# A macaron encoder block on 8 cores: modulation and first weights taken piece by piece at the start, norm products taken in pairs, and pairs of squares added on GpSimd in nine norms

## The reference, cut to what matters

```python
mod = (cc @ w_ada[l] + b_ada[l]).reshape(b, N_ADA, D_MODEL)
sh1, sc1, gt1, sh2, sc2, gt2, sh3, sc3, gt3 = [mod[:, i, None, :] for i in range(N_ADA)]
h = modulate(rms_norm(x, g_ffn1[l]), sh1, sc1)
x = x + 0.5 * gt1 * swiglu(h, w_ffn1_in[l], w_ffn1_out[l])
h = modulate(rms_norm(x, g_mix[l]), sh2, sc2)
x = x + gt2 * token_mix(h, w_in[l], ...)
h = modulate(rms_norm(x, g_ffn2[l]), sh3, sc3)
x = x + 0.5 * gt3 * swiglu(h, w_ffn2_in[l], w_ffn2_out[l])
```

## Time and profile before

| | us |
|---|---|
| three runs | 1567.2, 1570.02, 1849.1 |
| median | 1570.02 |
| the profiled execution: its time | 1571.91 |
| its span, slowest core (core 1) | 1570.4 |
| its span, fastest core (core 0) | 1558.5 |
| TensorE matmuls busy, of the span | 1497.1 |
| VectorE busy | 809.7 |
| ScalarE busy | 448.9 |
| GpSimd busy, DMA issues counted | 78.4 |

### The profile page before, as it was taken

How to read it: one execution, slowest core, us unless ns; L and a number is a source line. 1 busy time by engine, 2 the same in 40 slices (tenths; PEclk the granted TensorE clock), 3 DMA queues, 4 the chain that set the end, 5 groups by cost and what they waited for, 6 DMA issues and landing times.

```text
span 1570.4 us, 23354 instructions; the slowest of 8 cores (1558.5 to 1570.4 us)
## 1 busy us (share of the span) xinstructions
PE 1497.1 (95%) x8372; PEld 708.4 (45%) x8372; DVE 809.7 (52%) x1310; ACT 448.9 (29%) x636; POOL 78.4 (5%) x152
## 2 busy tenths in 40 slices
PE   2689999999999999988999999999999999999998
PEld 1334444444444444454564445444444444444443
DVE  2264527254272656667875568745544626253644
ACT  3361010101101036548665454523511010101010
POOL 1000000000101000000001000001000000000000
PEclk9789999999999999999999999999999999999999
DMA  9943352523515311240025345345232121211022
GB/s 198 204 110 54 54 88 41 95 41 54 95 27 93 63 18 64 81 98 5 11 68 88 61 94 110 68 69 111 43 54 41 31 51 27 48 27 28 1 107 107
DMA packets 24302, 107.12 MB, mean 68 GB/s; under 512 B 2816, under 2 KB 3072, under 8 KB 21760
## 3 DMA queue, kind: packets, MB, share of 16 engines
q0 software_dynamic: 21312, 75.67, 28.2%
q1 hardware_dynamic: 2880, 29.98, 5.3%
HBM read 168.71 MB, written 12.58 MB: 115 GB/s over the span
## 4 chain that ended last, share of the span: by engine, by line
PE 88%; DMA 6%; DVE 2%; ACT 2%; issue 1%; DVEq 0%; ACTq 0%; SPq 0%; POOLq 0%
PE ps L663 42%; PE ps L691 21%; PE ps L1016 7%; PE ps L826 4%; PE ps L1029 3%; PE ps L1048 3%; DMA arena<-w1i 3%; DMA arena<-x 2%; PE ps L962 1%; PE ps L809 1%; PE ps L872 1%; PE ps L908 1%; ACT arena L485 1%; DVE arena L497 1%; PE ps L580 1%
## 5 line engine op out<-in xcount | busy, mean ns | idle before, releaser
L663 PE MATMUL ps<-arena 128*128 128x512 bf16 x3152 | 694.7, 381 | 12.9 <-DMA arena<-w1i 4.8
L485 ACT ACTIVATE arena<-ps 128x512 bf16<-128x512 f32 (+3 forms) x426 | 268.7, 652 | 975.6 <-PE ps L663 810.3
L663 PEld LDWEIGHTS ps<-arena 128*128 128x128 bf16 x3152 | 308.1, 98 | 385.4 <-issue 23.1
L491 DVE TENSOR_TENSOR arena<-arena,ps 128x512 bf16<-128x512 bf16 x198 | 135.4, 687 | 510.8 <-PE ps L663 490.8
L497 DVE SCALAR_TENSOR_TENSOR arena<-ps,arena 128x512 f32<-128x512 f32 (+1 forms) x500 | 359.7, 748 | 72.2 <-ACT arena L485 23.1
L691 PE MATMUL ps<-arena 128*128 128x512 bf16 x1584 | 345.2, 379 | 2.1 <-DVE arena L497 1.1
L691 PEld LDWEIGHTS ps<-arena 128*128 128x128 bf16 x1584 | 154.3, 98 | 189.2 <-issue 6.3
L491 DVE TENSOR_TENSOR arena<-arena 128x1024 bf16<-128x1024 bf16 (+9 forms) x180 | 114.5, 656 | 39.8 <-ACT arena L485 33.2
L1016 PE MATMUL ps<-arena 128*128 128x512 bf16 x512 | 116.0, 379 | 0.0
L485 ACT ACTIVATE arena<-arena 128x512 f32<-128x512 f32 (+2 forms) x86 | 89.4, 1054 | 43.7 <-DVE arena L497 23.1
L497 DVE SCALAR_TENSOR_TENSOR arena<-arena 128x512 f32<-128x512 f32 (+1 forms) x112 | 79.2, 739 | 20.8 <-ACT arena L485 9.7
(11 more groups left out here) (60 smaller groups left out, 500.6 us busy)
## 6 DMA issues: line engine op xcount, KB each, us to landing
arena<-w_ada POOLq DMA_DIRECT2D x36, 512.0 KB, 7.3
arena<-w_gate POOLq DMA_DIRECT2D x24, 512.0 KB, 6.6
arena<-w1i POOLq DMA_DIRECT2D x22, 512.0 KB, 5.4
arena<-w3i POOLq DMA_DIRECT2D x22, 512.0 KB, 5.1
arena<-x SPq DMA_DIRECT2D x5, 2048.0 KB, 16.3
outT<-arena SPq DMA_DIRECT2D x8, 1024.0 KB, 3.9
arena<-w1o POOLq DMA_DIRECT2D x10, 512.0 KB, 5.3
arena<-w_kqvu POOLq DMA_DIRECT2D x10, 512.0 KB, 6.4
```

The costliest lines, as they stand in the source:

```text
L485: return e.activation(out=o, in_=i, func=func, scale=scale)
L491: return e.tensor_tensor(out=out() if callable(out) else out, in0=in0() if callable(in0) else in0, in1=in1() if callable(in1) else in1, op=op)
L663: ins = e.matmul(pst(t), lhsT=w[:, kt, :], rhs=hk(b, kt), start=(kt == 0), stop=(kt == 7))
```

## The change

Five things change.

1. The start. `w1i` piece 0 is asked for ahead of `w_ada` pieces 6 and 7 (`W1ST`). Each of the eight `w_ada` pieces has its own PSUM tile, bias addition and two-column result in `SS1`; the four shift pieces are copied, the four scale pieces get `(1 + scale) * g`. After each scale piece two tiles of block 0 are modulated (`norm_late(0, (2k, 2k+1))`). The first unit alternates its two accumulations over `kt`, so it can begin with the tiles that are there. Group 0 of feed-forward 1 takes the units of blocks 0 and 1 in turn for each weight, and the norm of block 2 stands behind the second weight. `x` of block 3 is asked for when `w1i` piece 2 has landed, not piece 3. One ring place is skipped.

2. `norm_apply` takes two `kt` in one `tensor_tensor` of 128x1024 (x times `rs`), into buffers twice as large, and then scale and shift for each `kt` in one instruction: `kt` 1, 4 and 7 on ScalarE, the other five on VectorE.

3. In the nine norms with `sub` above 0 (`fold`), each half of four squares is added pairwise by one GpSimd `tensor_tensor` of 128x1024 bf16, and each half is then summed by two matmuls in place of four.

4. The planner's model of DMA landing times (a function `drain`, not shown: while both queues have work, SP gets `SPSHARE` of the bandwidth `BW` and POOL the rest), and 15 of the 18 pairs of `RAMPS`.

5. The last 16 tokens of block 0's `H` are copied once (`HH`), and the pooling stage reads them there (not shown).

```diff
@@ -19,11 +19,11 @@
 CELL = 32
 
 SILU, EXP, LN, TANH = "silu", "exp", "ln", "tanh"
-RAMPS = {"v0a": (7.37, 11.91), "k0a": (10.15, 10.65), "k0b": (10.89, 11.92), "v0b": (12.65, 12.7),
-         "a0": (10.37, 12.62), "u0": (10.3, 12.44), "k3": (11.93, 12.42), "k4": (11.01, 13.72),
-         "v3": (15.11, 15.16), "v4": (12.45, 12.73), "q4": (13.4, 13.6), "a1": (14.08, 16.26),
-         "g0": (13.99, 15.41), "o0": (16.97, 17.82), "u1": (15.03, 18.92), "g1": (20.0, 20.5),
-         "n1": (18.67, 20.59), "o1": (21.26, 21.31)}
+RAMPS = {"v0a": (6.86, 12.16), "k0a": (10.15, 11.87), "k0b": (10.76, 11.77), "v0b": (12.6, 12.7),
+         "a0": (10.39, 12.64), "u0": (10.68, 12.89), "k3": (11.4, 12.42), "k4": (11.01, 14.15),
+         "v3": (15.11, 15.16), "v4": (13.29, 13.34), "q4": (13.4, 13.6), "a1": (14.08, 16.3),
+         "g0": (13.99, 15.41), "o0": (17.33, 18.34), "u1": (15.09, 18.95), "g1": (19.52, 20.02),
+         "n1": (16.9, 20.3), "o1": (21.22, 21.31)}
...
@@ -53,6 +53,8 @@
     LAT = 0.12
     PELAT = 0.22
     WINDOW = 96
+    BW = 315e3
+    SPSHARE = 0.64
...
-    TMPS = [[view(o + 2048 * i, F32, (TB,)) for i in range(2)] for o in (o_qt, o_expb)]
+    SS1 = view(o_aq, F32, (2, 4, 8))
+
+    def twin(o, o2):
+        v = view(o, F32, (TB,))
+        return bass.AP(v.tensor, v.offset, [list(v.ap[0]), [(o2 - o) // 4, 2], [1, TB]])
+    TMPS = [[twin(o_qt, o_qt + 2048), twin(o_expb + 8192, o_att + 8192)],
+            [twin(o_expb, o_expb + 2048), twin(o_expb + 8192, o_kq)]]
...
-    def norm_stats(b):
+    def norm_stats(b, fold=False):
         t = Tile()
         for hf in range(2):
             sq = H[:, b, 4 * hf:4 * hf + 4, :]
@@ -574,12 +596,19 @@
         for hf in range(2):
             sq = H[:, b, 4 * hf:4 * hf + 4, :]
 
-            def mm(e, hf=hf):
+            nq = 4
+            if fold:
+                nq = 2
+                lo, hi = H[:, b, 4 * hf:4 * hf + 2, :], H[:, b, 4 * hf + 2:4 * hf + 4, :]
+                sq = lo
+                tt(lo, lo, hi, ALU.add, [lo, hi], [lo], 2.3, eng="pool")
+
+            def mm(e, hf=hf, nq=nq):
                 ins = None
-                for kt in range(4 * hf, 4 * hf + 4):
-                    ins = e.matmul(pst(t), lhsT=ONES, rhs=hk(b, kt), start=(kt == 0), stop=(kt == 7))
+                for kt in range(4 * hf, 4 * hf + nq):
+                    ins = e.matmul(pst(t), lhsT=ONES, rhs=hk(b, kt), start=(kt == 0), stop=(kt == 3 + nq))
                 return ins
-            S.op("pe", mm, reads=[sq, ONES] + ([t] if hf else []), writes=[t], cost=mmc(4, 512))
+            S.op("pe", mm, reads=[sq, ONES] + ([t] if hf else []), writes=[t], cost=mmc(nq, 512))
         rs = RK[rk_pos[0] % 2]
         rk_pos[0] += 1
         act(rs, lambda: pst(t), AF.Ln, bias=EPSC[:, 0:1], reads=[t, EPSC], writes=[rs], cost=0.69, tset=LN)
@@ -587,16 +616,22 @@
         return rs
 
     def norm_apply(b, sub, rs):
-        for kt in range(8):
+        sc, sh = DER[:, 3 * sub, :], DER[:, 3 * sub + 1, :]
+        for kp in range(4):
             tb = TMPS[0 if sub < 2 else 1][tmp_pos[0] % 2]
             tmp_pos[0] += 1
-            stt(tb, xk(b, kt), DER[:, 3 * sub, kt:kt + 1], rs, ALU.mult, ALU.mult,
-                [xk(b, kt), rs, DER[:, 3 * sub, :]], [tb], 0.75)
-            if kt % 2 == 0:
-                act(hk(b, kt), tb, AF.Identity, bias=DER[:, 3 * sub + 1, kt:kt + 1], reads=[tb, DER[:, 3 * sub + 1, :]],
-                    writes=[hk(b, kt)], cost=0.72)
-            else:
-                ts(hk(b, kt), tb, DER[:, 3 * sub + 1, kt:kt + 1], ALU.add, [tb, DER[:, 3 * sub + 1, :]], [hk(b, kt)], 0.49)
+            xp = xblk(b)[:, 2 * kp:2 * kp + 2, :]
+            rb = bass.AP(rs.tensor, rs.offset, [list(rs.ap[0]), [0, 2], [1, TB]])
+            tt(tb, xp, rb, ALU.mult, [xp, rs], [tb], 1.1)
+            for kt in (2 * kp, 2 * kp + 1):
+                ti = tb[:, kt % 2, :]
+                s1, s2 = sc[:, kt:kt + 1], sh[:, kt:kt + 1]
+                if kt in (1, 4, 7):
+                    act(hk(b, kt), ti, AF.Identity, bias=s2, scale=s1, reads=[ti, sc, sh], writes=[hk(b, kt)], cost=0.8)
+                else:
+                    S.op("dve", lambda e, kt=kt, ti=ti, s1=s1, s2=s2: e.tensor_scalar(
+                        out=hk(b, kt), in0=ti, scalar1=s1, scalar2=s2, op0=ALU.mult, op1=ALU.add),
+                        reads=[ti, sc, sh], writes=[hk(b, kt)], cost=0.49)
 
     def norm_early(b):
         rs = norm_stats(b)
...
-    def norm_late(b):
-        for kt in range(8):
+    def norm_late(b, kts):
+        for kt in kts:
             xs = XSE[b][:, kt, :]
-            sc, sh = DER[:, 0, kt:kt + 1], DER[:, 1, kt:kt + 1]
+            cells = [SS1[:, 0, kt // 2, :], SS1[:, 1, kt // 2, :]]
+            sc, sh = [c[:, kt % 2:kt % 2 + 1] for c in cells]
             if kt % 3 == 1:
                 S.op("act", lambda e, kt=kt, xs=xs, sc=sc, sh=sh: e.activation(out=hk(b, kt), in_=xs, func=AF.Identity,
                                                                               bias=sh, scale=sc),
-                     reads=[xs, DER[:, 0:2, :]], writes=[hk(b, kt)], cost=0.8)
+                     reads=[xs] + cells, writes=[hk(b, kt)], cost=0.8)
             else:
                 S.op("dve", lambda e, kt=kt, xs=xs, sc=sc, sh=sh: e.tensor_scalar(
                     out=hk(b, kt), in0=xs, scalar1=sc, scalar2=sh, op0=ALU.mult, op1=ALU.add),
-                    reads=[xs, DER[:, 0:2, :]], writes=[hk(b, kt)], cost=0.49)
+                    reads=[xs] + cells, writes=[hk(b, kt)], cost=0.49)
 
     def norm(b, sub):
-        norm_apply(b, sub, norm_stats(b))
-
-    for c in range(8):
+        norm_apply(b, sub, norm_stats(b, sub > 0))
+
+    for c in range(6):
         ada_load(c)
+    W1ST = load("s", w1i[0])
+    ada_load(6)
+    ada_load(7)
     norm_early(0)
     norm_early(1)
-    t_ada = Tile()
     for c in range(8):
-        ada_mm(c, t_ada, 0)
-    ada_out(t_ada, 0, 8)
+        t = Tile()
+        ada_mm(c, t, c)
+        ada_out(t, c, 1)
+        src = MOD[:, 2 * c:2 * c + 2]
+        k = c % 4
+        dst = SS1[:, 1 - c // 4, k, 0:2]
+        if c < 4:
+            S.op("dve", lambda e, src=src, dst=dst: e.tensor_copy(out=dst, in_=src), reads=[src], writes=[dst], cost=0.17)
+        else:
+            g = CST[:, 80 + 2 * k:82 + 2 * k]
+            S.op("dve", lambda e, src=src, dst=dst, g=g: e.scalar_tensor_tensor(
+                out=dst, in0=src, scalar=1.0, in1=g, op0=ALU.add, op1=ALU.mult), reads=[src, CST], writes=[dst], cost=0.17)
+            norm_late(0, (2 * k, 2 * k + 1))
+    norm_late(1, range(8))
...
@@ -712,23 +763,33 @@
                     r.append(load(ring, wo_dd[wo_pos + q], None if full else 1, deps)[0])
                 return r
             if bmajor:
-                wl = [load(ring, wi_d[GSTART[g] + jl]) for jl in range(nk)]
+                head = [W1ST] if first and g == 0 else []
+                wl = head + [load(ring, wi_d[GSTART[g] + jl]) for jl in range(len(head), nk)]
                 wts = [w[0] for w in wl]
                 if lastg:
                     wos = wo_load()
                 if first and g == 0:
-                    norm_late(0)
-                    norm_late(1)
-                    for b, after in ((2, ADA[7][1]), (3, wl[3][1]), (4, wl[3][1])):
+                    for b, after in ((2, ADA[7][1]), (3, wl[2][1]), (4, wl[3][1])):
                         xl[b] = S.op("sp", lambda e, b=b: e.dma_start(out=XB[:, b - 1, :, :],
                                                               in_=x_d[b].rearrange("p (k t) -> p k t", k=8)),
                              writes=[XB[:, b - 1, :, :]], dma="d_x%d" % b, nbytes=1 << 21, deps=[after])
                     wos = wo_load([xl[2]])
                     for c in range(8, 12):
+                        if c == 11:
+                            rpos["s"] += 1
                         ada_load(c, [xl[3]])
                 for i, b in enumerate(blocks):
                     if g == 0 and first:
-                        if 0 < i < len(blocks) - 1:
+                        if i == 0:
+                            for jl in range(nk):
+                                unit(jl, 0, wts[jl])
+                                unit(jl, 1, wts[jl])
+                                if jl == 1:
+                                    norm(2, 0)
+                            continue
+                        if i == 1:
+                            continue
+                        if i < len(blocks) - 1:
```

52 lines of the change are left out of this document (35 added, 17 removed).

## The result

The changed kernel takes **1543.9 us** (median of four runs, 1543.7 to 1544.8), the kernel before, run beside it, 1568.1 (mean of three, 1567.2 to 1570.0). The ratio is 0.9846, with a 95% interval of 0.9827 to 0.9866: some 24 us less. Predicted was 1542, with a range of 1535 to 1552. The gain is under 2%, to which the prediction gave a chance of 0.77. Disturbed runs are left out of every time in this text, so that the kernel before has three runs here and e10 two.

The account below looks back on a forecast made before the run. TensorE, busy 95%, bounds the kernel, so only its idle time and removed matmuls give time: 16.0 + 7.8 + 3.0 + 1.6 = 28.4 us off 1571.9 gives 1543.5, less 1.9 over the median: 1542, range 1535 to 1552.

Parts of the forecast that it names:

- The start: Reordered weight pieces bring group 0's output products at 128.6 against 144.65: 16.0 us gained.
- The cores differ now mostly by when the start ends: Across cores: differences come mostly from when the start ends, which the new start evens out; no size given.
- the 17 that would have been wrong: Sign of a wrong prediction: TensorE idle more than 17 us from 560 to 1120.
- Rival B: Start: block 3's `x` lands no earlier, at 81, so the start gives 12 to 13: 1545; chance 0.15.
- The sums: Nine norms lose four matmuls each, 36 x 0.216 = 7.8 us, with 18 POOL additions in their place.
- Where the addition is hidden: End of feed-forward 1, blocks 0 to 2: an addition of 2.3 us is hidden with 0.3 to spare.
- The collision: VectorE's products of block 3's norm beside block 4's first addition: one might hold the other 1.2 us, K weight later, 1543.
- The norm products: VectorE's work per norm goes from 7.9 to 7.5 us, off the path except at the start: gain nothing.
- The mixer's order: Mixer: K weight's wait falls from 4.0 to 1.0, 3.0 gained, and one VectorE wait of 1.6 goes.
- the range of -6 to +9: Rest of the 17.5 us idle time from 560 to 1120: queue order changes bring between -6 and +9.
- E: Sums: the POOL addition takes 4.6 us, costing 10, 3 and 2 at three places: 1557; chance 0.05.
- F: Sums: POOL's addition is several times slower still, gain used up at about 6 us, 1588 at 8; chance 0.02.

Follow-up runs that it names:

- e10: The changed kernel with the additions only in the four norms ahead of feed-forward 2, none at the end of feed-forward 1: 1543.7 and 1544.4 us.
- e4: The kernel before with only the new start and the planner's new model of the DMA queues: 1552.0 us.
- e12: The changed kernel without the additions on POOL and with the old table of ramps: 1551.4 us.
- e2: The changed kernel without the additions on POOL, four matmuls per half again, order planned anew: 1545.6 us.
- e8: The changed kernel with block 3's `x` asked for when the fourth `w1i` piece has landed, not the third: 1545.4 us.
- e3: The changed kernel, same queue order, each of the 18 additions followed by a second one that the sum waits for: 1564.4 us.
- e9: The changed kernel without the additions in the norms of blocks 2 and 3 at the end of feed-forward 1: 1543.3 us.
- e1: The changed kernel, same queue order and additions kept, but four matmuls per half again in the nine norms: 1550.9 us.
- e6: The changed kernel with the norm products of before, order planned anew with the new table: 1554.8 us.
- e7: The changed kernel with a further POOL addition per first half, and norm products of blocks 0 to 2 behind the next evictions: 1547.6 us.

## Why the prediction was right

The total was right for partly wrong reasons. The prediction started from 1570.0 and took off 28.4 (1.9 of the 1571.9 were the profiled execution's own); the gain is some 24. The time is only 1.9 off because the runs here put the kernel before at 1568.1, and that part is luck. A chain of kernels, each with one thing more, gives the worth of the parts in that order, beside the prediction's terms:

| step | time | gives | predicted |
|---|---|---|---|
| before | 1568.1 | | |
| the new start (e4) | 1552.0 | 16.1 | 16.0 |
| the norm products (e12) | 1551.4 | 0.5 | 0 |
| the mixer's table (e2) | 1545.6 | 5.8 | 4.6 |
| the additions (changed kernel) | 1543.9 | 1.7 | 7.8 |

The rows stand on different chips, so the 0.5 is nothing and the 1.7 hardly more.

**The start: right in kind, over-sized by some 2, with two errors that cancel in part.** Block 2's `x` came at 62.3 and block 3's at 73.4, against 66.0 and 77.5: each was 4 us early, since `w_ada` piece 7 landed before 47.16 and not at 50.0. On the profiled core TensorE none the less got to the output products at 129.4, not 128.6, because the full matmuls were dearer: this core's granted clock was 0.94 from 60 to 100, a part of it at the lower of the two levels. Core 3 was at the lower level until 54 and at the full one after, and was there at 126.4. The sum compared this with 144.65, the latest core of before. By the median of the cores the start gives 13.8, by the latest 15.2. That the row of e4 has 16.1 is owed to the mixer, which gave 4.3 there, and is luck for this term. "The cores differ now mostly by when the start ends" held: they spread over 7.4 us at that point before and 4.2 after, and the spans over 11.9 and 5.5. The slowest core before was late for a second reason that the sentence leaves out, the clock in its mixer.

From 100 to 560 TensorE is idle 0.7 us in place of 0.3, and from 560 to 1120 15.8, under the 17 that would have been wrong. The early `w1o` piece, costed at nothing, issued at 49.64 and held nothing up. Rival B was ruled out by the landing at 73.4; e8 prices what it would have cost, at most 1.7 for 3.6.

**The sums: right in what was removed, wrong in what it cost.** The failing step is "Where the addition is hidden". It reckoned when a sum is ready, and that held: 2.12 us (predicted 2.3), no wait for POOL, and e3 shows the edge. But it counted only the sum's own wait. The additions also delayed block 2's norm products until after block 3's evictions had begun (3.0 us on TensorE, e9; in e2 on core 3 the products begin at 612.90 and the evictions at 623.07), and held VectorE itself at two places that TensorE waits for (2.3 us, e10). 7.0 in e1 less these is 1.7, but that it comes out so exactly is partly chance. Behind the start, the medians of TensorE's idle time are together 4.7 over e2's, and the five cores at the lower clock behind the 3.0 lose another 1.7 each; both come off 36 x 0.216 = 7.8.

**The collision: right in kind, wrong in place and victim.** I put it at block 4's first addition in feed-forward 1's last norm, with the K weight late by it. There (648.77) VectorE was reading PSUM and its evictions weren't held; beside block 4's second, at 652.22, a scale-and-shift of VectorE took 1.97 in place of 0.55. It struck TensorE at the pooling's products and the last norms, and mostly it was VectorE that waited, not POOL.

**The norm products: "Nothing" holds only without the rest.** e12 against e4 says 0.5, e6 says 10.9. I compared VectorE's busy time (7.5 against 7.9), but what counts here is how long the norm stands in a fixed queue and how it interlocks with the order around it.

**The mixer's order: the right sign, under-sized.** K's wait went from 4.0 to none (1.0 predicted). The table gives 5.8 and not 4.6, and 8.7 beside the additions. On cores without a stretch at the lower clock it gives 4.4 and 5.6, near the 4.6, but in many small waits and not in the two that I had named. The rest is the granted clock, for which the prediction had no term: it was in the range of -6 to +9 at best.

Rivals E and F fell with the 2.12 us. E's price can be checked against e3: at 4.24 it would have been 1557 by my reckoning, and was 1564.4, since the mixer lost 11.9 where I had expected 5.

## What to carry to other kernels

Removing matmuls from a full TensorE didn't pay in full here, because what replaced them pushed work of the evicting engine into a later, tighter place. So follow the norm's whole chain in that engine's queue, not only until the sum is ready. When parts share a planned order, undo each one both with the order held and with it planned anew; here the same 36 matmuls are worth 7.0 the one way and 1.7 the other. Look at the granted clock behind each long wait, on every core: here a wait of 3 us was followed by a loss of up to 2 more on five cores of eight. Cut two traces at the program's own events and not at fixed times.

## What the runs showed of the hardware

- GpSimd adds 128x1024 in bf16 in 2.12 us, VectorE in 0.69. Two such in a row on GpSimd are 2.24 and 1.98 on average (e3).
- GpSimd and VectorE shut each other out for whole instructions, and it isn't only VectorE's two-input products. A product of two SBUF inputs (128x512) took 2.42 in place of 0.69. A scale-and-shift with one float32 input in SBUF and a bf16 output took up to 2.16 in place of 0.55. The addition took 3.21 in place of 2.12 beside a product of 1.22. Evictions from PSUM ran beside it without loss (at 648.77, 0.75 each). The Trainium skill (SBUF — State Buffer, section "SBUF: two separate sides") names two SBUF inputs or a two-port mode as what takes part, and the first to start as the winner. The traces agree, save that at 1075.39 VectorE won while recorded 0.01 us later; that the scale-and-shift is in such a mode no run shows.
- The same wait is followed by a lower granted clock on some cores and not on others. Behind the 2.95 us for VectorE's evictions it was 0.50 for 3.4 us on five cores and 1.00 on three; behind e7's 2.2 at feed-forward 2 it was 0.50 for 3.4 us on three cores and 1.00 on five. The stage was 1.0 to 2.1 us longer on the five, and 1.7 us on the three.
- The cores of one run don't get the same clock at the start: on core 3 of the changed kernel it was 0.53 from 40 to 54 and 1.00 after, on core 7 1.00 from 40 to 60 and 0.94 to 100, with the same program:

```profile
54.00:100.00 46.00, 44.79 (x236) 20.64 (x234) 21.98 (x32) 31.18 (x34) 3.70 (x7) 1.00 0.92 213
```

```profile
60.00:100.00 40.00, 40.00 (x189) 17.68 (x188) 19.08 (x25) 27.15 (x29) 3.17 (x6) 0.94 0.90 203
```
